# A Hawk/HGRN2 block on eight cores: tiles 5 to 7 transpose keys and outputs by DMA, the last two row blocks get a buffer of their own, and ScalarE does fewer and shorter instructions

## What is computed

```
h = rms_norm(x) ; z = h @ w_in           # 8 column groups of 1024: xa ga q f i gb gm(2)
# branch A: causal conv of 4 taps, two block-diagonal gates, then a recurrence
a    = exp(-8 * gate_r * softplus(-lam)) ; mult = sqrt(1 - a*a)
h_t  = a_t h_{t-1} + mult_t * gate_i_t * x_t ; out_a = (h * silu(ga)) @ proj_a
# branch B: gated linear attention, 8 heads, keys and values of 128
f = lb + (1-lb) sigmoid(f_pre) ; k = 1 - f ; q = silu(q)
S_t = diag(f_t) S_{t-1} + k_t v_t^T ; o_t = S_t^T q_t          (computed by chunks)
o = rms_norm(o per head) * g ; out_b = (o * silu(gb)) @ proj_b
x = x + (sig(gm_a) * out_a + sig(gm_b) * out_b) @ w_out ; y = rms_norm(x) * final_g
```

## Time and profile before

| | |
|---|---|
| runs of the kernel before | 1404.45, 1404.53, 1434.55 us; median 1404.53 |
| profiled execution | 1405.57 us; span of its slowest core 1403.8 us |
| spans of the eight cores | 1398.9 to 1403.8 us |
| TensorE busy | 1357.8 us, 97% of the span |
| VectorE, ScalarE, POOL busy | 1020.6, 969.3, 412.9 us |
| granted TensorE clock, mean | 0.989 of full speed |

### The profile page before, as it was taken

The page is one execution under the profiler, slowest core; times in us unless marked ns, Lnnn a source line. Parts: engine busy times, 40 slices in busy tenths (PEclk is TensorE's granted clock), DMA queues, the critical chain, the costliest instruction groups (busy, mean ns, idle before and its releaser), DMA issues.

```text
span 1403.8 us, 26365 instructions; the slowest of 8 cores (1398.9 to 1403.8 us)
## 1 busy us (share of the span) xinstructions
PE 1357.8 (97%) x7330; PEld 655.6 (47%) x7330; DVE 1020.6 (73%) x1862; ACT 969.3 (69%) x2116; POOL 412.9 (29%) x759
## 2 busy tenths in 40 slices
PE   6978999999999999999999999999999999999996
PEld 2434444544445444444445444454444544444442
DVE  5577688677788776797767887678787777687564
ACT  4688777667777676687765678756787666678741
POOL 4334444335542344332332231112312012111200
PEclk9989999999999999999999999999999999999998
DMA  9999889998999999998999758755566355544452
GB/s 172 179 201 211 134 132 160 173 180 184 199 183 162 223 198 225 196 211 195 241 239 225 204 143 240 207 150 162 176 208 166 113 187 169 149 136 135 136 187 75
DMA packets 120669, 251.47 MB, mean 179 GB/s; under 512 B 13520, under 2 KB 13648, under 8 KB 119632
## 3 DMA queue, kind: packets, MB, share of 16 engines
q0 software_dynamic: 46368, 89.94, 41.6%
q1 hardware_dynamic: 74160, 159.86, 36.7%
HBM read 301.91 MB, written 37.75 MB: 242 GB/s over the span
## 4 chain that ended last, share of the span: by engine, by line
PE 91%; ACT 3%; issue 2%; DVE 2%; DMA 1%; POOL 0%; DVEq 0%; SPq 0%; ACTq 0%; POOLq 0%
PE PS L631 68%; PE PS L639 14%; PE PS L822 1%; PE PS L784 1%; PE PS L787 1%; PE PS L682 1%; PE PS L820 1%; PE PS L679 1%; PE PS L839 1%; PE PS L805 1%; DMA GA<-xt 1%; PE PS L589 1%; ACT BB L724 0%; ACT L724 0%; PE PS L555 0%
## 5 line engine op out<-in xcount | busy, mean ns | idle before, releaser
L631 PE MATMUL PS<-HT,WS 128*128 128x512 bf16 x3584 | 836.4, 380 | 5.7 <-DVE XR L864 1.9
L631 PEld LDWEIGHTS PS<-HT,WS 128*128 128x128 bf16 x3584 | 346.8, 98 | 386.3 <-issue 13.9
L621 POOL DMA_DIRECT2D WS<-wpk x305 | 167.4, 552 | 406.2 <-PE PS L631 275.2
L668 DVE SCALAR_TENSOR_TENSOR XC<-XA,PAR,XC 128x512 f32<-128x512 f32 x192 | 141.5, 743 | 1.5 <-DVE DP L906 0.4
L631 PE MATMUL PS<-SG,WS 128*128 128x512 bf16 x512 | 115.3, 379 | 0.0
L631 PE MATMUL PS<-SGB,WS 128*128 128x512 bf16 x512 | 114.8, 379 | 0.0
L530 POOL TENSOR_TENSOR SMALL<-SMALL,NHALF 128x4 f32<-128x4 f32 (+1 forms) x102 | 107.7, 1056 | 11.9 <-PE PS L631 0.4
L788 DVE TENSOR_TENSOR ATT<-PS,MSK 128x512 bf16<-128x512 f32 x64 | 44.2, 690 | 88.7 <-PE PS L787 80.6
L529 POOL TENSOR_SCALAR SMALL<-SMALL 128x4 f32<-128x4 f32 (+1 forms) x102 | 47.5, 465 | 190.5 <-ACT JNK L827 101.7
L810 ACT ACTIVATE SBF<-ST,G 128x128 bf16<-128x128 f32 x192 | 76.1, 396 | 22.8 <-DVE ST L814 17.3
L765 ACT ACTIVATE SGB<-PS 128x512 bf16<-128x512 f32 x64 | 38.2, 597 | 72.6 <-PE PS L631 69.3
(11 more groups left out here) (131 smaller groups left out, 2351.4 us busy)
## 6 DMA issues: line engine op xcount, KB each, us to landing
WS<-wbf SPq DMA_DIRECT2D x335, 256.0 KB, 3.6
WS<-wpk POOLq DMA_DIRECT2D x305, 256.0 KB, 10.8
XR<-x SPq DMA_DIRECT2D x60, 512.0 KB, 7.7
wbf<-WS SPq DMA_DIRECT2D x80, 256.0 KB, 8.9
...
HT<-xt POOLq DMA_DIRECT2D x7, 1024.0 KB, 12.4
WR<-wpk POOLq DMA_DIRECT2D x8, 256.0 KB, 17.7
...
```

Source lines behind the costliest of these rows:

```text
L621: P.emit("pool", lambda e: e.dma_start(out=W.phys[:, :], in_=dram["wpk"][k]), [], [W], dma_sem=s_ws[1], cost=560.0, nbytes=1 << 19, after= ...
L631: P.emit("pe", lambda e, k=k: e.matmul(ps.f32, W.phys[:, k * 128:(k + 1) * 128], src(k), start=(k == 0), stop=(k == 7)), [W] + src_bufs(k) ...
L668: dve(lambda e, k=k: e.scalar_tensor_tensor(C[:, :], X[:, k:k + TT], par(P_CW + 8 * k + m), C[:, :], ALU.mult, ALU.add), [bX, bC, b_PAR], ...
```

## The change

- **Keys and outputs of tiles 5 to 7.** `att_a` transposes K with one DMA from SBUF to SBUF, issued by ScalarE, into KTT; `att_c` transposes ONB by such a DMA into a new ring ONT of two, and VectorE's multiply reads that. TensorE's transposes, ScalarE's copy of KTT and the PSUM banks of both are gone in these tiles. The planner gives each such DMA 450 ns on ScalarE and a landing about 4.65 us behind it (200000 bytes at its rate of 308 bytes per ns, 2000 ns of latency and 2000 more), so 5.1 us from the start of the issue.
- **Lighter ScalarE work, in all tiles.** The head norm squares 128 x 512 in one instruction into a float32 scratch tile, and a VectorE reduction forms the four sums. In `lru_unit` the second exponential, of twice the exponent, becomes the square of the first.
- **Last row blocks.** Blocks 2 and 3 of tile 7 are loaded into the normed-input tile of tile 6, once its readers are done, instead of XR. Both are squared in halves; the final gain is multiplied in beside the norm; the last scaling is a multiply by the norm alone, three halves on ScalarE and one on VectorE; each half is stored for itself.
- **Planner.** Delays between engines become larger (270, 220, 180, 150 for 240, 150, 150, 120), and those within an engine 200, 180, 150 for 80.
- **Small things.** KEEP, the mask of the decay scan, becomes bf16. The scratch tile of the wide squares is merged into the one of the head norm, a ring of one. `RAWQ` and `RAWF` are empty lists, so that their branches are never taken.

```diff
+DT = 5
+LAST_X = [(NTILES - 1, 2), (NTILES - 1, 3)]
+RAWQ = []
+RAWF = []
...
-    HOP = {"pe": 240.0, "act": 150.0, "dve": 150.0, "pool": 120.0, "sp": 100.0}
+    HOP = {"pe": 270.0, "act": 220.0, "dve": 180.0, "pool": 150.0, "sp": 100.0}
+    OWN = {"pe": 0.0, "act": 200.0, "dve": 180.0, "pool": 150.0, "sp": 0.0}
...
-            return 0.0 if a.eng == "pe" else 80.0
+            return self.OWN[a.eng]
...
-        KEEP = sb("KEEP", [128, TT], F32)
+        KEEP = sb("KEEP", [128, TT], BF16)
...
-        r_SQJ = ring("SQJ", 1, [128, D], BF16)
-        r_JNK = ring("JNK", 1, [128, 512], BF16)
+        r_JNK = ring("JNK", 1, [128, 512], F32)
...
+        r_ONT = ring("ONT", 2, [128, 4, 128], BF16)
...
-            act(lambda e: e.activation(M[:, :], A[:, :], AF.Exp, scale=dp(m), bias=dp(m)), [bA, b_DP], [bM], 700.0, T_LE)
             act(lambda e: e.activation(A[:, :], A[:, :], AF.Exp, scale=dp(48 + m), bias=dp(48 + m)), [bA, b_DP], [bA], 700.0, T_LE)
+            act(lambda e: e.activation(M[:, :], A[:, :], AF.Square), [bA], [bM], 520.0)
...
-            p1, pa = Bank("s"), Bank("s")
-            L, bL, _ = r_KTT.take()
+            L, bL, i = r_KTT.take()
             T, bT, _ = r_ATT.take()
-            for n in range(4):
-                ape(lambda e, n=n: e.transpose(p1.b16[:, CS[n]], K[:, CS[n]], IDB[:, :]), [bK, b_IDB], [p1])
-            act(lambda e: e.activation(L[:, :, :].rearrange("p h d -> p (h d)"), p1.b16[:, 0:512], AF.Copy), [p1], [bL], 490.0, bias=AB)
+            if tile < DT:
+                p1 = Bank("s")
+                for n in range(4):
+                    ape(lambda e, n=n: e.transpose(p1.b16[:, CS[n]], K[:, CS[n]], IDB[:, :]), [bK, b_IDB], [p1])
+                act(lambda e: e.activation(L[:, :, :].rearrange("p h d -> p (h d)"), p1.b16[:, 0:512], AF.Copy), [p1], [bL], 490.0, bias=AB)
+            else:
+                P.emit("act", lambda e: e.dma_start(out=L[:, :, :], in_=K[:, :], transpose=True), [bK], [bL],
+                       dma_sem=s_kt[i], cost=450.0, nbytes=200000, lat=2000.0, bias=AB)
+            pa = Bank("s")
...
-            for n in range(4):
-                act(lambda e, n=n: e.activation(J[:, CS[n]], po.f32[:, CS[n]], AF.Square, accum_out=SMALL[:, c0 + n:c0 + n + 1]), [po], [bJ, bs], 400.0, bias=AB)
+            act(lambda e: e.activation(J[:, :], po.f32, AF.Square), [po], [bJ], 520.0, bias=AB)
+            dve(lambda e: e.tensor_reduce(SMALL[:, c0:c0 + 4], J[:, :].rearrange("p (h v) -> p h v", h=4), mybir.AxisListType.X, ALU.add), [bJ], [bs], 600.0, bias=AB)
...
-            p2 = Bank("s")
-            for n in range(4):
-                ape(lambda e, n=n: e.transpose(p2.b16[:, CS[n]], O[:, n, :], IDB[:, :]), [bO, b_IDB], [p2])
-            dve(lambda e: e.scalar_tensor_tensor(SGB[z][:, m, :], p2.b16[:, 0:512], par(P_HG), SGB[z][:, m, :], ALU.mult, ALU.mult),
-                [p2, b_PAR, b_SGB[z][m]], [b_SGB[z][m]], 670.0, bias=AB)
+            if tile < DT:
+                p2 = Bank("s")
+                for n in range(4):
+                    ape(lambda e, n=n: e.transpose(p2.b16[:, CS[n]], O[:, n, :], IDB[:, :]), [bO, b_IDB], [p2])
+                dve(lambda e: e.scalar_tensor_tensor(SGB[z][:, m, :], p2.b16[:, 0:512], par(P_HG), SGB[z][:, m, :], ALU.mult, ALU.mult),
+                    [p2, b_PAR, b_SGB[z][m]], [b_SGB[z][m]], 670.0, bias=AB)
+            else:
+                V, bV, i = r_ONT.take()
+                P.emit("act", lambda e: e.dma_start(out=V[:, :, :], in_=O[:, :, :].rearrange("p h v -> p (h v)"), transpose=True), [bO], [bV],
+                       dma_sem=s_ot[i], cost=450.0, nbytes=200000, lat=2000.0, bias=AB)
+                dve(lambda e: e.scalar_tensor_tensor(SGB[z][:, m, :], V[:, :, :].rearrange("p h v -> p (h v)"), par(P_HG), SGB[z][:, m, :], ALU.mult, ALU.mult),
+                    [bV, b_PAR, b_SGB[z][m]], [b_SGB[z][m]], 670.0, bias=AB)
...
-                live["x", tile, j] = x_load(tile, j)
+                live["x", tile, j] = x_load(tile, j) if (tile, j) not in LAST_X else x_last(tile, j)
             X, bX, i = live["x", tile, j]
+            bX = bX[h] if (tile, j) in LAST_X else bX
             sl = slice(h * 512, h * 512 + 512)
             ps = group_tm(live["wo", tile, h], lambda k: GB[:, k, j * 128:(j + 1) * 128], lambda k: [b_GB[k]])
             dve(lambda e: e.scalar_tensor_tensor(X[:, sl], ps.f32, 0.5, X[:, sl], ALU.mult, ALU.add), [ps, bX], [bX], 615.0)
-            if tile == NTILES - 1 and j == 3:
-                c0 = 40 + j + h
+            if (tile, j) in LAST_X:
+                c0 = 32 + 2 * (j - 2) + h
+                bm = b_SML[j - 2]
                 Q, bq, _ = r_JNK.take()
-                act(lambda e: e.activation(Q[:, :], X[:, sl], AF.Square, scale=D ** -0.5, accum_out=SMALL[:, c0:c0 + 1]), [bX], [bq, b_SML[h]], 530.0)
+                act(lambda e: e.activation(Q[:, :], X[:, sl], AF.Square, scale=D ** -0.5, accum_out=SMALL[:, c0:c0 + 1]), [bX], [bq, bm[h]], 530.0)
+                if h == 0:
+                    pool(lambda e: e.tensor_scalar(SMALL[:, c0:c0 + 1], SMALL[:, c0:c0 + 1], EPS, None, ALU.add), [bm[0]], [bm[0]], 300.0)
+                dve(lambda e: e.tensor_tensor(X[:, sl], X[:, sl], FNG[:, sl], ALU.mult), [bX, b_FNG], [bX], 615.0)
                 if h == 1:
-                    r, bs, bh = SMALL[:, c0:c0 + 1], b_SML, bl("Y", 2)
-                    pool(lambda e: e.tensor_scalar(r, r, SMALL[:, c0 - 1:c0], EPS, ALU.add, ALU.add), bs, bs[1:], 300.0)
-                    pool(lambda e: e.tensor_tensor(r, r, NHALF[:, 0:1], ALU.pow), bs[1:] + [b_NH], bs[1:], 280.0)
+                    r, r0 = SMALL[:, c0:c0 + 1], SMALL[:, c0 - 1:c0]
+                    pool(lambda e: e.tensor_scalar(r, r, r0, None, ALU.add), bm, bm[1:], 300.0)
+                    pool(lambda e: e.tensor_tensor(r, r, NHALF[:, 0:1], ALU.pow), bm[1:] + [b_NH], bm[1:], 280.0)
                     for g in range(2):
-                        sg = slice(g * 512, g * 512 + 512)
-                        dve(lambda e, sg=sg: e.scalar_tensor_tensor(X[:, sg], X[:, sg], r, FNG[:, sg], ALU.mult, ALU.mult), [bX, bs[1], b_FNG], [bh[g]], 690.0)
-                        out_ops.append(P.emit("sp", lambda e, sg=sg: e.dma_start(out=yv[tile, j, :, sg], in_=X[:, sg]), [bh[g]], [], dma_sem=s_last[g], cost=450.0, nbytes=1 << 18))
+                        sg, bg = slice(512 * g, 512 * g + 512), live["x", tile, j][1][g]
+                        if j == 3 and g == 0:
+                            dve(lambda e, sg=sg: e.tensor_scalar(X[:, sg], X[:, sg], r, None, ALU.mult), [bg, bm[1]], [bg], 455.0)
+                        else:
+                            act(lambda e, sg=sg: e.activation(X[:, sg], X[:, sg], AF.Copy, scale=r), [bg, bm[1]], [bg], 500.0)
+                        out_ops.append(P.emit("sp", lambda e, sg=sg: e.dma_start(out=yv[tile, j, :, sg], in_=X[:, sg]), [bg], [], dma_sem=s_last[2 * (j - 2) + g], cost=450.0, nbytes=1 << 18))
             elif h == 1:
...
+        def x_last(tile, j):
+            p = (tile + 1) % 2
+            g = LAST_X.index((tile, j))
+            T = HT[p][:, 4 * g:4 * g + 4, :].rearrange("p c t -> p (c t)").bitcast(F32)
+            b = bl("XL%d_" % g, 2)
+            P.emit("sp", lambda e: e.dma_start(out=T, in_=xv[tile, j]), writes=b_HT[p][4 * g:4 * g + 4] + b, dma_sem=s_xl[g], cost=450.0, nbytes=1 << 19)
+            return T, b, 0
```

More of the change, by code:

```diff
@@ L230, in arrange @@
         dma_free = 0.0
[L231 removed]
+        q_free = {"sp": 0.0, "act": 0.0}
         for op in self.all:
@@ L307, in arrange @@
                 dma_free = max(dma_free, now) + took
-                if e == "sp":
-                    sp_free = max(sp_free, now) + min(2 * took, dma_free - now)
-                    op.end = min(sp_free, dma_free) + self.DMA_LAT + op.lat
+                if e != "pool":
+                    q_free[e] = max(q_free[e], now) + min(2 * took, dma_free - now)
+                    op.end = min(q_free[e], dma_free) + self.DMA_LAT + op.lat
                 else:
@@ L496, in _build @@
         b_TST, b_G3, b_BREF = bl("TST", 8), bl("G3", 8), bl("BREF", 8)
-        b_SMX, b_SMF, b_SMH, b_SML = Buf("SMX"), bl("SMF", 4), bl("SMH", 4), bl("SML", 2)
+        b_SMX, b_SMF, b_SMH, b_SML = Buf("SMX"), bl("SMF", 4), bl("SMH", 4), [bl("SML%d" % i, 2) for i in range(2)]
         s_c = [sem("ld_c%d" % i) for i in range(5)]
@@ L505, in _build @@
         s_ht = [sem("ld_h%d" % i) for i in range(2)]
-        s_last = [sem("st_l%d" % i) for i in range(2)]
+        s_kt = [sem("kt%d" % i) for i in range(2)]
+        s_ot = [sem("ot%d" % i) for i in range(2)]
+        s_xl = [sem("ld_xl%d" % i) for i in range(2)]
+        s_last = [sem("st_l%d" % i) for i in range(4)]
         out_ops = []
@@ L711, in q_group @@
             Q, bQ, _ = r_QT.take()
-            act(lambda e: e.activation(Q[:, :], ps.f32, AF.Silu), [ps], [bQ], 490.0, T_SILU)
+            if (tile, m) in RAWQ:
+                B, bB, _ = live["bb", tile, m] = r_BB.take()
```

(12 more changed lines are left out.)

17 lines of the change are left out of this document (10 added, 7 removed).

## The result

The changed kernel takes 1395.35 us (median), the kernel before 1404.74 in the same runs: ratio 0.9936, interval 0.992 to 0.9952. It is 9.4 us faster, half of the 18.6 that were forecast. In some executions of any of these kernels one pair of cores or more runs at a lower granted clock and takes longer, which the ratios of e9 and e12 still contain in part, so that the text gives for these two the time of their undisturbed runs as well. The profiled execution took 1395.09 us, its slowest core 1393.5 us, against 1405.57 and 1403.8.

A forecast was written before the change was run, and what follows sets the result against it. TensorE was taken to bound the middle, with waits for VectorE's keys in the first tile and a 13.5 us end. 1405.6 - 10.6 - 5.2 - 2.8 = 1387.0, or 1386 us against the runs' median; range 1374 to 1400.

The forecast's parts named there:

- rival B: VectorE, ScalarE or landings of 6 to 7 us open small TensorE waits; 1393 to 1407 us, chance 0.17.
- Transposes off TensorE: Tiles 5 to 7: 192 TensorE transposes at 0.055 us each removed, where TensorE has no idle time; -10.6 us.
- VectorE heavier: 64 added reductions, 44 us on VectorE, hidden by TensorE's queue; 0, up to +5 us in the first tile.
- four dense banks of 1.73 us each ahead: Work queued on TensorE that was to hide the added VectorE reductions; without it a pair costs 1.4 us.
- a sign of being wrong that the prediction named: VectorE's reductions appearing as what TensorE's banks wait for.
- DMA transposes, 0: Tiles 5 to 7: ScalarE has room for the issues, landings of 4.0 us fit the planner's 5.1; no cost.
- An issue on ScalarE longer than 1.3 us: Sign of being wrong for the DMA transposes in tiles 5 to 7; 1.31 us was the worst SP issue.
- The slack of 7.1 us: Last tile: spare time before the first `pb` group needs the last head's gates; two landings use 4.8 us.
- ScalarE lighter: First tile: lighter norm squares shorten ScalarE's chain before the keys TensorE waits for; -2.8 us, bounds 0 and -16.
- The end, -5.2: After the last matmul: last add 4.7 us earlier, scaling 0.6 less, 0.1 taken back; between -3.5 and -6 us.
- The planner's new order: Every engine's order made anew; counted as 0, worth some 3 us either way.

The follow-up runs named there:

- e9: Changed kernel with four squares on ScalarE, DMA transposes issued by SP, last two head pairs on TensorE, reordered end: 0.9898 of the kernel before; undisturbed 1388.6 to 1389.5 us.
- e12: Kernel before with only the new head norm (one wide square, VectorE reduction) and the bf16 KEEP: 1.0116 of the kernel before; undisturbed 1416.6 to 1420.8 us.
- e3: Changed kernel with the old head norm (four squares with sums on ScalarE, no VectorE reduction): 0.9924 of the kernel before.
- e1: Changed kernel with all transposes of K and ONB back on TensorE: 0.9994 of the kernel before.
- e5: Changed kernel with the 48 DMA transposes issued by SP in place of ScalarE: 0.9918 of the kernel before, the control 0.9953.
- e6: Changed kernel with the last two head pairs of tile 7 transposed by TensorE again: 0.9928 of the kernel before, the control 0.9953.
- e11: Changed kernel with the second exponential back in place of the square: 0.9959 of the kernel before.
- e13: Changed kernel with a reordered end (block 2 scaled by VectorE, POOL's sum one instruction) and block 2 stored by one DMA: end 9.8 us; no ratio given.
- e4: Changed kernel with the end of the kernel before (last blocks in the ring of three, old last norm): 0.9976 of the kernel before.
- e7: Changed kernel with the planner told 1250 ns of ScalarE per DMA transpose instead of 450: 0.9972 of the kernel before, the control 0.9953.
- e10: Changed kernel with the planner's smaller delays of before (240, 150, 150, 120 and 80): 0.9955 of the kernel before.

## Why the prediction was wrong

The sign was right and the two gains came, but the size was twice the measured one, because two terms were put at 0 that are not 0, and the end was over-estimated. 1395.35 lies in the stated range and in what rival B gave (1393 to 1407, chance 0.17), and B, the gain going back in small waits, is what happened.

- *Transposes off TensorE, -10.6*: right, 12.1 less busy. The Trainium skill's 390 ns ("VectorE: DVE Perf Modes", "The three transpose paths") do not hold inside a stream, where a transpose adds 55 ns; its 1309 ns by DMA, times four, would be an estimated 5.2 us, and the trace has medians of 3.4 and 4.3 us with the issue.
- *VectorE heavier, 0, "cover: TensorE's queue, with four dense banks of 1.73 us each ahead"*: this step failed. The cover is not four banks where what TensorE needs is not a bank but VectorE's product: GB for the output groups. There VectorE was already at 94% in a slice of 35 us before the change. Measured: three waits of 3.5 us in the changed kernel, gone without the reductions (2.8 us of gaps in the cores' median, 6.7 and 3.9 with and without), and a kernel 11 us slower with the reductions alone (e12). The average, 73% to 76%, hid it. This was a sign of being wrong that the prediction named, but for an operand in place of a bank. The rest of the middle's 5.0 us, the waits for GB above all, is in e3 too and stays open.
- *DMA transposes, 0*: this step failed in the last tile. In the middle the late landings show no wait in the profiled core. In the last tile the DMA transposes cost 3 us of gaps (6.2 against 3.0 in e1), and some 3.5 us of clock behind them. Of the gaps 1.4 go with the issue on ScalarE ahead of a Silu (e5), and 2.5 go when the last two pairs are back on TensorE (e6): the wait for XR falls from 2.0 to 0.6 us and that for QT from 2.1 to 0.3. Why XR comes later with DMA transposes no run shows. An issue on ScalarE longer than 1.3 us was to be a sign of being wrong, and six were; the one ahead of the Silu was not among them, 1.21 us were enough. The slack of 7.1 us that I computed is that of the outputs, and these were in time; I had not asked about TensorE's stop at the start of the pair.
- *ScalarE lighter, -2.8*: near in size (-2.6 on the slowest core, -1.6 in the median), by luck in part, since the reason was wrong. The wait for keys fell by 3.2 us. Of that the head norm, on which the sum was built, gave 0.1 in the new order (e3), and the square for the exponential 1.3 (e11); it shortens the Ln and Exp run at the end of which the keys stand. The rest came with the new order, and new waits for weights took part of it back.
- *The end, -5.2*: -3.2. Of the add coming early, 4.7 us, all but 0.2 is there; the row from which I took the base is that of the slowest core, at 13.5 us, where the median is 12.0. What was added is seen in the end's timeline:

```profile
1383.30 0.72 ACT L913 ACTIVATE HT<-HT,SMALL 128x512 f32<-128x512 f32 x1 [1.88 <-POOL SMALL L907]
1383.46 0.68 DVE L895 SCALAR_TENSOR_TENSOR HT<-PS,HT 128x512 f32<-128x512 f32 x1
1383.93 0.61 ACT L900 ACTIVATE JNK<-HT 128x512 f32<-128x512 f32 x1
...
1385.15 0.61 ACT L900 ACTIVATE JNK<-HT 128x512 f32<-128x512 f32 x1
...
1386.03 0.77 POOL L906 TENSOR_SCALAR SMALL<-SMALL 128x1 f32<-128x1 f32 x1 [0.52 <-ACT JNK L900]
...
1387.61 0.72 ACT L913 ACTIVATE HT<-HT,SMALL 128x512 f32<-128x512 f32 x1 [1.75 <-POOL SMALL L907]
```

The last add ends at 1384.14, and its square starts only at 1385.15: ScalarE had stood waiting for block 2's norm ahead of two squares. I had priced that at 0.1; it is 0.9. POOL's sum is 0.5 longer. The last scaling ends at 1388.33, 5.1 us before the end, against 4.4 before. Of those 0.7, 0.2 is that both halves are ready at nearly the same time and SP issues one store behind the other, the last at 1388.61; 0.4 is that this store lands in 2.5 us, where the last one landed in 2.1 before. Why it lands later is open; the fourth store is not it (e13).

*The planner's new order, "some 3 us either way"*: right as a size and wrong as a term of 0. Edits that touch one place moved the gaps elsewhere by 1 to 3 us (e4, e7, e10). That is as much as several of the differences above, which is why the named waits, and not the sums, carry the argument.
